# Delta net of a decoder layer: sample tile as first chunk, gates and stores inside the token projection, output norms per pair

## The chip, the cores and the metric

One core of a Trainium2 chip runs the whole program. The metric is device time in microseconds for one execution. The kernel before takes 1897.65 us (median of three runs, 1895.38 to 1902.17).

## The reference, cut to what matters

The program computes one layer of a hybrid decoder for a prompt of 1024 tokens and a sample group of 8 sequences with 8 tokens each: RMS norm, one input projection, three mixers (sparse attention, a gated delta net, a state space mixer), the output projection and an MLP. The change touches the delta net and the projection ahead of it:

```python
def deltanet_mix(qkv, a, b, z, conv_buf, s0, conv_w, a_log, dt_bias, norm_w):
    ...
    beta = jax.nn.sigmoid(b.astype(f32))
    g = -jnp.exp(a_log.astype(f32)) * jax.nn.softplus(a.astype(f32) + dt_bias.astype(f32))
    o, s_new = gated_delta_chunked(q, k, v, g, beta, s0.astype(f32))
    o = rmsnorm(o, norm_w) * jax.nn.silu(z.astype(f32).reshape(B, L, DN_HEADS, DN_DV))
...
def gated_delta_chunked(q, k, v, g, beta, s0):
    ...
    gc = jnp.cumsum(g...)                       # per chunk
    decay = jnp.where(tri, jnp.exp(gc_i - gc_j), 0.0)
    a_mat = jnp.where(strict, (beta k) @ k^T * decay, 0.0)
    sol = lax.linalg.triangular_solve(a_mat + eye, rhs, left_side=True, lower=True)
    u, w = sol[..., :dv], sol[..., dv:]
    def step(S, xs):
        v_new = u_i - w_i @ S
        o_i = (q_i * exp(g_i)) @ S + a_qk @ v_new
        S = S * exp(g_last) + (k_i * exp(g_last - g_i))^T @ v_new
        return S, o_i
```

(Index bookkeeping is written out as products here.) There are four heads of 64 channels. The prompt starts from a zero state; each sample sequence starts from its own state, which is also returned.

## The kernel before, in words

The rows of all tokens lie in nine tiles: tiles 0 to 7 are the prompt, 128 rows each, and tile TS = 8 holds the 64 rows of the sample group. The program is a row of blocks; within a block every engine runs its own list of instructions, ordered by hand, with semaphores between them, and a block ends on all engines together. The blocks that matter here:

- `project` called by `token_projection` (name `kvp`, lines 394 to 396 for the matmuls, 522 for the copies): a product of the normalised input with four chunks of 264 weight columns; the 36 units (chunk, tile) take 24 matmuls of three kinds each. Columns 0 to 767 are keys and values of the attention (`m.kv`), the other 288 are `m.small`: attention gates (24), the delta net's a and b (4 each) and z (256). ScalarE copies the even units, VectorE the odd ones. Behind its last copy ScalarE's queue issues the stores of the keys and values (lines 529 to 536, function `stores`), and the block ends when they are issued.
- `delta_net` (from line 1140). SyncE loads parameters and constant tables (1250 to 1255), then the page table and the 16 pages of the attention's cache (1262), and once all tiles' rows are read the sample states (1265). Gates (1337 to 1348, 1444 to 1462) take z through SiLU, softplus and exponentials for all tiles at once, with cumulative sums on TensorE (1649 to 1653). Then tile by tile: decay rows (1687), rows turned out of the convolution's result (1664), normalised and scaled (`normalise` 1471 to 1478 on VectorE, `scale` 1297 to 1303 on GpSimd), turned (1675), products of keys and queries (1703), decayed (1507).
- The triangular solve is done in levels, for pairs of tiles, `PAIRS = [(0, 1), (2, 3), (4, 5), (6, 7), (TS,)]`: seven levels for a full pair, three (`SLEVELS`) for the sample tile, whose blocks are 8 x 8. A level is `lower` on TensorE, a copy on ScalarE, `joined` on TensorE, an update on VectorE (1541 for level 0, 1561 for level 6, 1553 for the sample tile). Between these steps of pair p, the next pair is prepared, and the chained part of pair p - 1 runs, tile by tile: `w_products` (1766), `v_products` (1776 to 1785), `s_products` (1791, 1796), `next_state` (1521), `take_o` (1528).
- Behind the last pair: `finish` squares, sums, takes the root by a power on GpSimd (1333), multiplies with the norm's weight, the root and SiLU(z), for tiles 0 to 5, 6 and 7, and TS; the sample tile's masked products with its eight states (1836 to 1860); `turn_rows` (1823) and `keep_rows` (1430) put the result into `m.mixT`.

In the trace the names `dn_...` are tiles of the delta net, `tokens` holds `m.kv` and `m.small`, and `ps` are the banks of the matmul memory.

## Time and profile before

| | us |
|---|---|
| median of three runs | 1897.65 |
| profiled execution, its own time | 1897.29 |
| its span in the trace | 1895.4 |
| PE busy in the span | 1690.9 (89%) |
| DVE, ACT, POOL busy | 876.1, 517.3, 322.0 |
| mean granted clock of TensorE | 0.906 |

The engines are PE (TensorE, matmuls), PEld (its weight loads), DVE (VectorE), ACT (ScalarE), POOL (GpSimd) and SP (SyncE, which only issues transfers here); a q behind the name is the queue, where transfers are issued. Granted clock 1.0 is 2.4 GHz and 0.5 is 1.2 GHz. Times inside the trace count from the start of the span. A row of a timeline gives start, duration, engine, line, operation, what it writes and reads with shapes, how often; brackets give the idle time before it and what ended it, where "issue" means that the engine waited for nothing the profile shows. Busy times are sums over a stage; an engine can be idle without cost when another one sets the pace.

### The profile page before, as it was taken

How to read it: one execution, taken by the hardware profiler on the slowest of the kernel's cores; microseconds unless marked ns; L12 is line 12 of the kernel's file. 1: busy time of each engine (PE TensorE's matmuls, PEld its weight loads, DVE VectorE, ACT ScalarE, POOL GpSimd, SP SyncE). 2: the span in 40 equal slices, each digit the busy share in tenths (PEclk: the TensorE clock that was granted, in tenths of full speed). 3: DMA queues.
4: the chain of work that ended last, by engine and by line, in shares of the span. 5: the costliest groups of instructions: out<-in, count | busy, mean ns of one | idle time of the engine just before them, and what ended most of it. 6: DMA issues, size and time to landing. Idle time of an engine off the chain costs nothing. (4 is left out here: it accounts for less than half of the span.)

```text
span 1895.4 us, 34835 instructions
## 1 busy us (share of the span) xinstructions
PE 1690.9 (89%) x15219; PEld 1521.4 (80%) x15219; DVE 876.1 (46%) x1742; ACT 517.3 (27%) x1043; POOL 322.0 (17%) x291
## 2 busy tenths in 40 slices
PE   6999889648886676689998999999999999999998
PEld 5999889647775565467778999999999999999996
DVE  5950631033534321667754264444444444444447
ACT  6212421022211221566653042111111111111112
POOL 2010020022211000567760001111111111111110
PEclk8999999857865655799999999999999999999999
DMA  4010110240000202000003101111111111111102
GB/s 149 24 37 12 59 46 24 71 131 3 4 31 2 76 1 88 1 1 2 1 2 117 45 23 56 45 45 45 45 45 45 45 45 45 45 45 45 45 23 95
DMA packets 28498, 81.14 MB, mean 43 GB/s; under 512 B 6922, under 2 KB 15226, under 8 KB 23066
## 3 DMA queue, kind: packets, MB, share of 16 engines
q1 hardware_dynamic: 25810, 73.03, 11.5%
q10 hardware_dynamic: 1976, 4.92, 0.7%
q8 instruction: 119, 1.95, 0.4%
q0 software_dynamic: 560, 0.97, 0.2%
q14 instruction: 33, 0.27, 0.0%
HBM read 70.89 MB, written 10.12 MB: 43 GB/s over the span
## 5 line engine op out<-in xcount | busy, mean ns | idle before, releaser
L394 PE MATMUL ps<-mlp_mix_hi,mlp_w_hi 128*128 128x360 f32 (+1 forms) x768 | 252.5, 329 | 0.0
L396 PE MATMUL ps<-mlp_mix_hi,w_lo 128*128 128x360 f32 (+1 forms) x768 | 252.3, 329 | 0.0
L395 PE MATMUL ps<-mixT_lo,mlp_w_hi 128*128 128x360 f32 (+1 forms) x768 | 251.5, 328 | 0.0
L2650 DVE TENSOR_TENSOR x<-x,ps 128x512 f32<-128x512 f32 (+1 forms) x288 | 180.6, 655 | 137.7 <-PE ps L396 137.0
L2630 POOL TENSOR_TENSOR mlp_rect<-mlp_rect 128x360 f32<-128x360 f32 (+1 forms) x96 | 77.5, 807 | 775.4 <-ACT mlp_rect L2572 775.4
L394 PE MATMUL ps<-mlp_w_hi,mlp_hid_hi_lo 128*128 128x512 f32 x512 | 202.1, 395 | 0.0
L396 PE MATMUL ps<-mlp_w_hi,mlp_hid_lo 128*128 128x512 f32 x512 | 202.1, 395 | 0.0
L395 PE MATMUL ps<-w_lo,mlp_hid_hi_lo 128*128 128x512 f32 x512 | 202.1, 395 | 0.0
L2572 ACT ACTIVATE mlp_rect<-ps 128x360 f32<-128x360 f32 (+1 forms) x96 | 45.5, 474 | 554.2 <-PE ps L396 551.3
L2212 POOL TENSOR_SCALAR pa_probs<-pa_probs,pa_fac 128x640 f32<-128x640 f32 (+7 forms) x96 | 158.7, 1666 | 187.9 <-DVE pa_fac L2139 187.9
L2690 DVE TENSOR_TENSOR mlp_hid_lo<-mlp_rect,mlp_hid_hi_lo 128x368 fp32r<-128x368 f32 (+1 forms) x64 | 53.1, 830 | 234.8 <-ACT mlp_hid_hi_lo L2578 234.8
L394 PEld LDWEIGHTS ps<-mlp_mix_hi,mlp_w_hi 128*128 128x128 f32 x768 | 144.5, 188 | 0.8
L395 PEld LDWEIGHTS ps<-mixT_lo,mlp_w_hi 128*128 128x128 f32 x768 | 144.4, 188 | 0.7
L396 PEld LDWEIGHTS ps<-mlp_mix_hi,w_lo 128*128 128x128 f32 x768 | 144.1, 188 | 0.0
L396 PEld LDWEIGHTS ps<-mlp_w_hi,mlp_hid_lo 128*128 128x128 f32 x512 | 96.5, 188 | 22.5
L395 PEld LDWEIGHTS ps<-w_lo,mlp_hid_hi_lo 128*128 128x128 f32 x512 | 96.5, 188 | 22.5
L394 PEld LDWEIGHTS ps<-mlp_w_hi,mlp_hid_hi_lo 128*128 128x128 f32 x512 | 96.4, 188 | 22.4
L2224 ACT ACTIVATE pa_probs<-pa_probs,pa_nm 128x640 f32<-128x640 f32 (+7 forms) x128 | 92.5, 728 | 9.9 <-DVE pa_nm L2128 9.8
L2640 DVE TENSOR_TENSOR w_lo<-w_raw,mlp_w_hi 128x2048 fp32r<-128x2048 f32 x36 | 82.4, 2288 | 25.0 <-ACT mlp_w_hi L2547 25.0
L394 PE MATMUL ps<-kvp_whi,h_hi 128*128 128x264 f32 x288 | 82.8, 287 | 6.3 <-DVE kvp_wlo L476 6.3
L2071 PEld LDWEIGHTS ps<-ident,pa_probs 128*128 128x128 f32 x528 | 57.4, 142 | 37.5 <-issue 33.1
L2071 PE MATMUL ps<-ident,pa_probs 128*128 128x128 f32 x528 | 70.4, 280 | 18.7 <-issue 15.7
(491 smaller groups left out, 3411.5 us busy)
## 6 DMA issues: line engine op xcount, KB each, us to landing
w_raw<-in_w_up SPq DMA_DIRECT2D x16, 1024.0 KB, 4.9
w_raw<-in_w_down SPq DMA_DIRECT2D x16, 1024.0 KB, 4.9
feat_raw<-in_w_feat SPq DMA_DIRECT2D x12, 512.0 KB, 3.6
uT<-in_w_token SPq DMA_DIRECT2D x4, 1056.0 KB, 5.0
ck<-in_cache_nsa SPq DMA_DIRECT2D x16, 256.0 KB, 2.9
w_raw<-in_w_out SPq DMA_DIRECT2D x4, 1024.0 KB, 7.2
x<-in_x_prompt SPq DMA_DIRECT2D x4, 1024.0 KB, 8.5
out_y_p<-x SPq DMA_DIRECT2D x8, 512.0 KB, 2.6
```

The source lines that it names most:

```text
L394: pe.matmul(out, lhs[0], rhs[0], start=first, stop=False)
L395: pe.matmul(out, lhs[0], rhs[1], start=False, stop=False)
L396: return pe.matmul(out, lhs[1], rhs[0], start=False, stop=last)
L2071: last = pe.transpose(m.ps[:, 4 + st % TURNS, (2 * s + g) * P:(2 * s + g + 1) * P], probs[:, slot(e, g), col:col + P], m.ident[:])
L2212: last = pool.tensor_scalar(probs[:, x, o:o + w], probs[:, x, o:o + w], fac[:, x, b:b + 1], None, ALU.mult)
L2224: act.activation(probs[:, x, o:o + w], probs[:, x, o:o + w], ACT.Exp, bias=nm[:, x, b, pieces(i)[j][1]:pieces(i)[j][1] + 1], scale=-1.0, a ...
L2572: act.activation(rect[:, (rank[u] - 1) % 2, :w], m.ps[:, bank_of(u), :w], ACT.Relu).then_inc(rectified, 1)
L2630: pool.tensor_tensor(part, part, part, ALU.mult).then_inc(rect_squared, 1)
L2640: dve.tensor_tensor(w_lo[:, s, :], w_raw[:, s, :], w_hi[:, s, :], ALU.subtract).then_inc(w_lo_made, 1)
L2650: dve.tensor_tensor(part, part, bank, ALU.add).then_inc(done, 1)
L2690: dve.tensor_tensor(hid_lo[:, g % 2, f, o:o + w], part, hi, ALU.subtract).then_inc(hidden_lo, 1)
```

## The change

`TOKEN_ORDER = (3, 0, 1, 2)`: the token projection takes its last chunk of columns first, so that a, b and most of z are there after nine units. A new class `DeltaGates` does all gate work between the projection's units: loads by GpSimd, `scalar` at units 10, 12 and 18, `vector` at 9, 10, 12, 14 and 17, the five sums on TensorE behind unit 16, in bank 7, which the projection gives up. GpSimd multiplies SiLU(z) with the norm's weight there. The stores move to SyncE's list and follow the copies they need; the twelve large ones of the prompt become three. In the delta net, chunk j = 0 is the sample tile and j = 1 to 8 are tiles 0 to 7, `PAIRS = [(0,), (1, 2), (3, 4), (5, 6), (7, 8)]`. The sample tile's masks, products and state update stand in the steps of pair 1; its states and masks lie in the memory of the attention's cache, whose loads wait until the states are stored. `finish` becomes `finish_sums`, `roots` and `finish_rows`, once per pair.

```diff
+TOKEN_ORDER = (3, 0, 1, 2)
...
     def stores(sp, evac):
-        sp.wait_ge(evac[0], (len(units) + 1) // 2)
-        sp.wait_ge(evac[1], len(units) // 2)
-        for t in range(TS):
-            sp.dma_start(m.kv_prompt[t * P:(t + 1) * P, :], m.kv[:, t, 0:512]).then_inc(stored, 16)
-            if t >= TS // 2:
-                sp.dma_start(m.win_prompt[(t - 4) * P:(t - 3) * P, :], m.kv[:, t, 512:768]).then_inc(stored, 16)
...
+        sp.dma_start(m.win_sample[:, 0:PAST, :], m.cache_win).then_inc(stored, 16)
+        for t0 in (0, 4):
+            units_done(2 * TILES + t0 + 3)
+            sp.dma_start(m.kv_prompt[t0 * P:(t0 + 4) * P, :].rearrange("(t p) n -> p t n", p=P), m.kv[:, t0:t0 + 4, 0:512]).then_inc(stored, 16)
+        units_done(3 * TILES - 1)
+        sp.dma_start(m.kv_sample, m.kv[:NB * NQ, TS, 0:512]).then_inc(stored, 16)
+        units_done(3 * TILES + TS - 1)
+        sp.dma_start(m.win_prompt.rearrange("(t p) n -> p t n", p=P), m.kv[:, TS // 2:TS, 512:768]).then_inc(stored, 16)
+        units_done(len(units) - 1)
         for b in range(NB):
+            sp.dma_start(m.win_sample[b, PAST:PAST + NQ, :], m.kv[b * NQ:(b + 1) * NQ, TS, 512:768]).then_inc(stored, 16)
...
+class DeltaGates:
...
+    def tensor(self, pe, u):
+        if u != 16:
+            return
+        pe.wait_ge(self.loaded, 16 * self.LOADS)
+        pe.wait_ge(self.g_ready, 1)
+        pe.matmul(bank[:, 0:32], C["upto"][:], g, start=True, stop=True)
...
-        names = ["ones", "ones_s", "upto", "upto_s", "level32", "eye32", "seq_row"]
+        names = ["level32", "eye32"]
...
-        Ss = flat_hT[:, :NB * 2 * P].rearrange("p (b c n) -> p b c n", b=NB, c=2)
+        Ss = flat_ck[:, 0:2048].rearrange("p (b c n) -> p b c n", b=NB, c=2)
...
-        PAIRS = [(0, 1), (2, 3), (4, 5), (6, 7), (TS,)]
-        STEPS = [7, 7, 7, 7, SLEVELS]
+        PAIRS = [(0,), (1, 2), (3, 4), (5, 6), (7, 8)]
+        STEPS = [SLEVELS, 7, 7, 7, 7]
...
             @block.sync
+                sp.dma_start(Ss, m.state_dn).then_inc(s_in, 16)
...
+                sp.wait_ge(ss_ready, H * SP_CHUNKS)
                 for h in range(2):
                     half = slice(64 * h, 64 * h + 64)
+                    for c in range(2):
+                        sp.dma_start(m.dn_sample[half, :, c], Ss[half, :, c, half]).then_inc(stored, 16)
+                sp.wait_ge(stored, 16 * 4)
                 sp.wait_ge(pages_loaded, 16)
                 for j in range(NB * PAGES):
...
             @block.gpsimd
+                def roots(p):
+                    pool.wait_ge(osq, p + 1)
+                    pool.tensor_tensor(part(T1), part(T0), m.minus_half[:, :H * (t1 - t0)], ALU.pow).then_inc(orn, 1)
...
             @block.vector
                     at_step(p, 2, level, [(next_state, c), (take_o, c), (normalise, b)])
+                    if p >= 2:
+                        finish_sums(p - 2)
+                    at_step(p, 3, level, [(take_o, 0 if p == 1 else None), (decayed, a)])
+                    if p == 1:
+                        decay_sample()
                     at_step(p, 4, level, [])
+                    spread_blocks(p)
+                    if p == 1:
+                        next_sample(0)
+                        next_sample(1)
                     at_step(p, 5, level, [(decayed, b), (next_state, d), (take_o, d)])
+                    if p == 1:
+                        next_sample(2)
                     at_step(p, 6, level, [])
+                    if p == 1:
+                        next_sample(3)
+                    if p >= 2:
+                        finish_rows(p - 2)
...
             @block.tensor
+                def sample_s(i):
+                    if i:
+                        pe.wait_ge(ss_ready, H * i)
...
+                for s, piece in enumerate(((w_products, 0), (sample_v,), (sample_o,), (), (sample_s, 0), (sample_s, 1), (sample_s, 2))):
+                    lower(1, s)
+                    if piece:
+                        piece[0](*piece[1:])
+                    at_step(1, s, joined, then)
```

How the instructions move, at three places. First, the border between the token projection and the delta net. Before, on ScalarE, the last stores, the end of the block, and the first gate step:

```order
L532 DMA out_kv_s<-tokens 64x512
L534 DMA out_win_s<-tokens 8x256 x8
L536 DMA out_win_s<-in_cache_win 8x4x16384
L438 UNCONDITIONAL_BRANCH
L1335 UNCONDITIONAL_BRANCH
L1337 ACTIVATE tokens<-tokens 128x9x256
L1339 ACT_TABLE_LOAD
L1339 ACTIVATE dn_gate<-dn_gate 128x36
```

Now, on SyncE, from the projection's weight loads to the delta net's first loads:

```order
L445 DMA uT<-in_w_token 128x2112 x3
L534 DMA out_win_s<-in_cache_win 8x4x16384
L537 DMA out_kv_p<-tokens 128x4x512 x2
L539 DMA out_kv_s<-tokens 64x512
L541 DMA out_win_p<-tokens 128x4x256
L544 DMA out_win_s<-tokens 8x256 x8
L438 UNCONDITIONAL_BRANCH
L1388 UNCONDITIONAL_BRANCH
L1392 DMA dn_level<-in_const 128x160
L1392 DMA dn_eye<-in_const 128x32
L1393 DMA ck<-in_state_dn 128x2048
L1395 DMA ck<-in_const 128x512
```

The stores are off ScalarE; on SyncE all but the last two groups stand ahead of the last units' copies, and only two tables are loaded before the sample states (`ck<-in_state_dn`).

Second, TensorE's products for the sample tile. Before, they stand at the end of the delta net, between two groups of turned output rows (`ident,dn_o`):

```order
L1766 MATMUL ps<-dn_TT,dn_kbg 64x64 x4
L1823 MATMUL ps<-ident,dn_o 128x128 x12
L1836 MATMUL ps<-dn_vb,dn_TT 64x64 x4
L1840 MATMUL ps<-mixT_raw,dn_B 64x128 x16
L1846 MATMUL ps<-mixT_raw,dn_TT 64x128 x16
L1854 MATMUL ps<-dn_vnew,dn_AT 128x128 x16
L1860 MATMUL ps<-dn_vnew,dn_aqkT 64x64 x4
L1823 MATMUL ps<-ident,dn_o 128x128 x4
L1823 MATMUL ps<-ident,dn_o 128x64 x2
```

Now they stand in the first levels of pair 1 (`dn_T,dn_B` are the levels, `ident,mixT_raw` and `ident,dg_gate` rows and decay rows of the next pair):

```order
L1860 MATMUL ps<-dn_featT 128x128 x8
L1878 MATMUL ps<-ident,dn_B 32x32 x32
L1928 MATMUL ps<-dn_TT,dn_kbg 64x64 x4
L1822 MATMUL ps<-ident,mixT_raw 128x128 x6
L1844 MATMUL ps<-ident,dg_gate 128x128 x8
L1878 MATMUL ps<-dn_T,dn_B 32x32 x32
L1967 MATMUL ps<-dn_vb,dn_TT 64x64 x4
L1972 MATMUL ps<-ck 64x128 x16
```

The sample tile's first products follow level 0, and the sixteen with the states follow level 1 of pair 1. The rest follows in the same way, one group for each level.

Third, GpSimd in pair 2, with the semaphores that each instruction waits for. Before, in the pair (4, 5), the next two tiles are scaled one right after the other:

```order
L1297 TENSOR_TENSOR dn_qg<-dn_qk,dn_gate 128x256 [waits dn_turned,dn_gexp,dn_normed]
L1301 TENSOR_TENSOR dn_kdec<-dn_qk,dn_gate 128x256 [waits dn_sprod,dn_wprod]
L1303 TENSOR_TENSOR dn_kbg<-dn_kb,dn_gate 128x256 [waits dn_kb_made]
L1297 TENSOR_TENSOR dn_qg<-dn_qk,dn_gate 128x256 [waits dn_turned,dn_gexp,dn_normed]
L1301 TENSOR_TENSOR dn_kdec<-dn_qk,dn_gate 128x256 [waits dn_sprod,dn_wprod]
L1303 TENSOR_TENSOR dn_kbg<-dn_kb,dn_gate 128x256 [waits dn_kb_made]
L1320 TENSOR_TENSOR dn_B<-dn_ATc,dn_level 128x5x128 [waits dn_bt,dn_packed_a]
```

Now, in pair (3, 4):

```order
L1430 TENSOR_TENSOR dn_qg<-dn_qk,dg_gate 128x256 [waits dn_turned,dn_normed]
L1434 TENSOR_TENSOR dn_kdec<-dn_qk,dg_gate 128x256 [waits dn_sprod,dn_wprod]
L1436 TENSOR_TENSOR dn_kbg<-dn_kb,dg_gate 128x256 [waits dn_kb_made]
L1461 TENSOR_TENSOR dg_gate<-dg_gate,minus_half 128x4 [waits dn_osq]
L1430 TENSOR_TENSOR dn_qg<-dn_qk,dg_gate 128x256 [waits dn_turned,dn_normed]
L1434 TENSOR_TENSOR dn_kdec<-dn_qk,dg_gate 128x256 [waits dn_sprod,dn_wprod]
L1436 TENSOR_TENSOR dn_kbg<-dn_kb,dg_gate 128x256 [waits dn_kb_made]
```

The power for the output norm of pair 0 (`dg_gate,minus_half`, which waits for VectorE's sums) stands between the scaling of the two tiles. In pair 3 the same instruction stands there with eight columns.

## Rows read from the trace of the kernel before

**Rows 1.** Table by stage: us; busy PE, PEld, DVE, ACT, POOL; PE clock, DMA share, GB/s.

```profile
364.00:377.00 13.00, 0.43 (x4) 0.21 (x2) 0.42 (x1) 0.16 (x1) 0.00 (x0) 0.65 0.73 257
377.00:397.00 20.00, 2.68 (x10) 2.43 (x10) 2.85 (x14) 6.99 (x12) 2.87 (x5) 0.50 0.48 155
397.00:422.00 25.00, 15.07 (x142) 13.11 (x143) 9.66 (x22) 4.81 (x15) 9.44 (x10) 0.57 0.41 125
...
459.00:499.00 40.00, 33.69 (x1112) 30.44 (x1106) 18.29 (x46) 9.54 (x27) 9.51 (x10) 0.84 0.02 4
...
537.00:580.00 43.00, 35.09 (x1009) 31.58 (x1006) 11.90 (x32) 6.92 (x20) 3.66 (x5) 0.58 0.10 34
...
602.00:645.00 43.00, 18.98 (x131) 16.69 (x132) 24.13 (x39) 3.74 (x11) 8.73 (x3) 0.68 0.07 14
```

**Rows 2.** Timeline of ScalarE: start, us, what; in brackets the idle time before.

```profile
372.11 3.12 ACTq L534 DMA_DIRECT2D out_win_s<-tokens  x8
...
376.84 2.12 ACT L1337 ACTIVATE tokens<-tokens 128x2304 f32<-128x2304 f32 x1 [14.89 <-PEq L438]
...
644.88 1.28 ACT L1909 ACT_TABLE_LOAD   x1 [1.70 <-PEq L2851]
```

**Rows 3.** Timeline of SyncE's queue.

```profile
380.60 4.60 SPq L1255 DMA_DIRECT2D dn_eye<-in_const  x1
...
387.70 0.34 SPq L1258 DMA_DIRECT2D pages<-in_page_table  x1
390.58 17.24 SPq L1262 DMA_DIRECT2D ck<-in_cache_nsa  x16
...
539.15 0.34 SPq L1265 DMA_DIRECT2D mixT_raw<-in_state_dn  x1
```

**Rows 4.** Timeline of VectorE, end of the token projection and first gate step.

```profile
364.46 0.42 DVE L522 COPY tokens<-ps 64x264 f32<-64x264 f32 x1 [5.37 <-PE ps L396]
388.95 0.20 DVE L1444 TENSOR_TENSOR dn_gate<-tokens,dn_dtb 128x36 f32<-128x36 f32 x1 [24.07 <-DMA dn_normw<-in_norm_w]
```

**Rows 5.** Timeline of TensorE, a gate sum and the decay rows.

```profile
394.95 0.61 PE L1653 MATMUL ps<-dn_gm,dn_ones 64*128 64x32 f32 x2
...
397.12 3.78 PE L1687 MATMUL ps<-ident,dn_gate 128*128 128x128 f32 x16 [1.56 <-ACT dn_egl_s L1348]
```

**Rows 6.** Timeline of VectorE: first levels, last levels, last state step.

```profile
422.00 0.41 DVE L1541 TENSOR_TENSOR dn_T<-dn_eye,ps 128x256 f32<-128x256 f32 x1
...
459.30 0.41 DVE L1541 TENSOR_TENSOR dn_T<-dn_eye,ps 128x256 f32<-128x256 f32 x1
...
537.11 0.41 DVE L1541 TENSOR_TENSOR dn_T<-dn_eye,ps 128x256 f32<-128x256 f32 x1
...
579.52 0.68 DVE L1561 TENSOR_SCALAR dn_TT<-ps 64x512 f32<-64x512 f32 x1 [3.06 <-PE ps L1753]
...
591.75 0.35 DVE L1553 TENSOR_TENSOR dn_T<-dn_T,ps 64x256 f32<-64x256 f32 x1
...
599.59 1.16 DVE L1521 SCALAR_TENSOR_TENSOR dn_S<-dn_S,dn_gate,ps 64x64 f32<-64x64 f32 x4 [5.96 <-PE ps L1791]
```

**Rows 7.** Timeline of TensorE: a turn, a stop, a chained tile, sample products.

```profile
518.56 0.63 PE L1675 MATMUL ps<-ident,dn_qk 128*128 128x128 f32 x4
...
546.62 0.33 PE L1746 MATMUL ps<-dn_T,dn_U 32*32 32x32 f32 x8 [3.08 <-issue]
...
593.32 1.12 PE L1766 MATMUL ps<-dn_TT,dn_kbg 128*64 128x128 f32 x8 [1.76 <-DVE dn_S L1521]
...
619.94 5.65 PE L1840 MATMUL ps<-mixT_raw,dn_B 128*64 128x128 f32 x32
```

**Rows 8.** Page of the profile, DMA queues: packets, MB, share of 16 engines.

```profile
q8 instruction: 119, 1.95, 0.4%
```

**Rows 9.** Timeline of GpSimd: the scaling of a tile, the power over eight columns.

```profile
516.67 0.85 POOL L1297 TENSOR_TENSOR dn_qg<-dn_qk,dn_gate 128x256 f32<-128x256 f32 x1 [12.69 <-DVE dn_qk L1471]
...
620.45 2.01 POOL L1333 TENSOR_TENSOR dn_gate<-dn_gate,minus_half 128x8 f32<-128x8 f32 x1 [9.76 <-DVE dn_gate L1611]
```

More of the change, by code:

```diff
@@ new lines, in next_sample @@
+                def next_sample(i):
+                    dve.wait_ge(ss_prod, i + 1)
+                    upd = m.ps[:, W0, :].rearrange("p (b c n) -> p b c n", b=2, c=2)
+                    for h in range(H):
+                        half = slice(64 * (h % 2), 64 * (h % 2) + 64)
+                        blk = Ss[half, 2 * i:2 * i + 2, h // 2, half]
+                        dve.tensor_tensor(blk, blk, upd[half, :, h // 2, half], ALU.add).then_inc(ss_ready, 1)
+                dve.wait_ge(tables, 16 * len(names))
@@ L1653, in _, with rows_of @@
-                pe.matmul(bank[:, 128:160], C["ones"][:64, :], gm[:].rearrange("p b h -> p (b h)"),
-                          start=True, stop=True).then_inc(sums, 1)
-                pe.wait_ge(gexp, 4)
-                def rows_of(k):
-                    n = ROWS[k]
-                    if k:
-                        pe.wait_ge(feat_out, 3 * k)
+                def rows_of(j):
+                    n, t = rows_in(j), tile(j)
+                    low, high = row_banks(j)
+                    if j >= 2:
+                        pe.wait_ge(feat_out, 3 * j)
@@ L1709, in lower @@
                     if s == 0:
-                        pe.wait_ge(b_ready, sum(len(x) for x in PAIRS[:p + 1]))
+                        pe.wait_ge(b_ready, PAIRS[p][-1] + 1)
                     else:
@@ L1806, in _ @@
+                sample_s(3)
+                for p in range(2, len(PAIRS)):
                     (a, b), (c, d) = following(p), chained(p)
```

910 lines of the change are left out of this document (511 added, 399 removed).

## The prediction

> **What bounds the kernel now.** I read the table by stage first, then each engine's timeline at the stage borders, then the waits and the DMA queue. TensorE is the engine of the whole program, but the change touches only the stretch from the end of the token projection to the end of the delta net, 364 to 645 us, and there it is not saturated: in the table by stage [rows 1] PE is busy 0.43 us of the 13 between 364 and 377, 2.68 of the next 20, 15 of the next 25, then 34 and 35 of the 40 and 43 us of two of the pairs of tiles, and 19 in the last 43. So five pieces follow one another, each with its own limit, and I cost each by itself.
>
> First, 364 to 397. ScalarE's queue still has to issue the projection's stores; eight small ones of them alone take 3.12 us, and its first delta net instruction stands at 376.84 [rows 2]. Only then does SyncE begin the small loads; one of them holds its queue for 4.60 us [rows 3], and VectorE waits for the last of the gate parameters until 388.95 [rows 4]. Then come the gates, and TensorE's first real step, the decay rows, starts at 397.12 [rows 5]. Second, 397.12 to 422.00: the first two tiles are prepared with nothing beside them. Third, the pairs: the marks "first level of a pair" stand at 422.00, 459.30 and 537.11, and the last level of the last full pair at 579.52 [rows 6]. Each pair is a loop of hand-offs (TensorE, ScalarE, TensorE, VectorE), and TensorE is busy some 34 us of it. Fourth, 579.52 to 645: the sample tile's levels, its masks and products and the output norms, one behind the other; VectorE is the busier engine there, 24 of the 43 us after 602 [rows 1].
>
> **The start, -23.6 us.** The stores leave ScalarE. SyncE now issues all but the window rows of the last chunk before the last unit; what remains behind it are the eight small stores, 3.1 us [rows 2]. The gate sums on TensorE move into the projection, where it never idles: five groups like the row of 0.61 us at the half clock [rows 5], at full clock about 1.5 us in all, so the last unit ends at 366.0 instead of 364.5, its copy at 366.4. Then 3.1 us of stores, 0.8 to leave the block (ScalarE's eight stores end at 375.23, one more follows, and its next instruction starts at 376.84 [rows 2]), 0.8 for two table loads like the 0.34 us one, and 2.5 until they land; a small load lands in under 2.9 us when nothing is queued before it (387.70 to 390.58) [rows 3]. TensorE starts at 373.5 instead of 397.12. The gates' vector and scalar steps, the seven loads that GpSimd issues and its product with the norm's weight cost nothing: VectorE is idle 5.37 us between two copies of the projection [rows 4], ScalarE as long, and TensorE has seven banks ahead. If that cover failed, the price would be the 8.2 us from 388.95 to 397.12 again [rows 4, 5].
>
> **The first tiles, +18.3 us.** Before, two tiles take 24.9 us (397.12 to 422.00). Now the sample tile comes first and tiles 0 and 1 are prepared around its three levels. The engines' busy times of this stretch add to 39 us over four engines [rows 1], so it is a chain of hand-offs, little overlapped. I add two thirds of one tile's 12.4 us for the half-height sample tile, 8.3, and 10 for its three levels, which before ran from just after 579.52 to 591.75 beside chained products [rows 6]. That gives 43.2, so the first full pair starts at 416.7, 5.3 us earlier than before. Lower bound: the two fully overlap, 33; upper: nothing overlaps, 48.
>
> **The four full pairs, +8.3 us.** Before, they take 157.5 us: 37.3 (nothing chained behind it), 77.8 for the middle two, 42.4 for the last [rows 6].
> - The pair that carries the sample tile. It replaces a middle pair's two chained tiles. The sample's products are longer: 5.65 us for one of three groups [rows 7], and about 15 for all (the 19 us of TensorE in the last stage [rows 1] less the turning of finished rows); two chained tiles take about 10 at that clock. VectorE gets masks, a decay and 16 additions instead of two state updates, some 5 us more of work in a pair where it is busy 18 of 40 us; but the four state chunks pass through one bank, so each waits for the one before. 38.9 + 5.6 = 44.5. It could be 41 (all in idle time) or 50 (the chunks in full on the path).
> - The next pair carries the cache loads. Before, SyncE issued them from 390.58 over 17.24 us [rows 3], when TensorE had few instructions to fetch. Now they wait for the sample states, whose place they take, and start as this pair does. The nearest row is the one large load before inside the pairs, at 539.15: TensorE then stands still for 3.08 us before 546.62, ended by "issue", that is, with no semaphore missing [rows 7]. Bounds: nothing, or one such stop for each instruction packet; the page of the profile counts 119 instruction packets [rows 8] for TensorE's 30,438 weight loads and matmuls, so one each 256; 17.24 us of a pair hold some 480 matmuls [rows 1], four packets, 12.3 us. Each piece is a quarter of that load in bytes, so I take 4. **A rule against this:** the Trainium skill (Runtime: NRT & Kernel Launch, Instruction fetch mechanics) says that fetching is hidden by the rate at which instructions are issued. By that rule the term is nothing and the sum 4 us lower; the 3.08 us row speaks against it.
> - Output norms. GpSimd now raises the sums of squares to a power between the scaling of a pair's two next tiles, and VectorE makes the sums just before. For eight columns the power takes 2.01 us [rows 9]. In the third pair VectorE's step before the sums ends at 517.4 (0.7 after the scaling starts at 516.67); with 1.6 of sums (two passes over 512 columns of some 0.7 us each) and the power, the scaling (0.85 us) [rows 9] would end at 522, and TensorE's turn of that tile stands at 518.56 [rows 7]: 3.4 us late. In a pair that runs slower there it is less, down to nothing. I take 1 us for the pair with the sample's four columns and 2 for the next. The second half of each norm falls behind the last level, where VectorE waits for TensorE anyway.
> - The last pair has nothing to prepare: 42.4 less the 3.08 us stop and 2.8 for the sample tile's own preparation, 36.5.
> The sum is 44.5 + (38.9 + 0.5 + 4 + 1) + (38.9 - 0.5 + 2) + 36.5 = 165.8; the 0.5 is the first middle pair's excess over the mean. So the last level starts at 582.5.
>
> **The tail, -40.6 us.** Before, 65.4 us from 579.52 to 644.88 [rows 2, 6]. Now, after the last level (0.7): two chained tiles of 7.4 each (593.32 to 600.75, the end of the state step) [rows 6, 7]; the last output's copy, sums, power and products, 0.4 + 1.6 + 2.0 + 1.4 with gaps, 5.6; turning and copying two tiles 2.0; leaving the block 1.7 [rows 2]. That is 24.8, and the earlier tiles turn beside it. The sample tile's levels, its products, two of three norms and the wait for its state are gone from here.
>
> **Sum.** -23.6 + 18.3 + 8.3 - 40.6 = -37.6 us. The profiled execution took 1897.29 us, 0.4 below the median, which gives 1859.7, so I predict 1860. Nothing after the block changes; the cache pages land long before their first use.
>
> **Rivals.**
> 1. Better than that, 1850: the three sample levels hide in the preparation (-5), and the loads and the power stop nothing (-5). For it: PE idles 10 of 25 us while the first tiles are prepared. Against: the 3.08 us row. Chance 0.20.
> 2. The small stores and the window store still stand before the tables: SyncE's queue stalls as it did for 4.60 us [rows 3], and the tables land behind half a megabyte of window rows, 2 us at the 257 GB/s of the stores before [rows 1]. The start gains 17 and the time is 1866. This is the case in which the change doesn't take the stores off the path. Chance 0.07.
> 3. The clock stays low. In the last pair before, the mean granted clock is 0.58 (between its levels of 1.2 and 2.4 GHz) and the pair takes 42.4 us although half of its preparation is missing; at 0.84 the first of the full ones takes 39 to 40 [rows 1]. With the clock low, a full pair costs 42.4 less the stop of 3.1, plus about 8 for the preparation that is missing there: 47. Three of them in place of 44.5, 44.4 and 40.4 add 11.7, which gives 1871. Chance 0.10.
> 4. **Slower:** every one of the 16 cache loads stops TensorE for 3.08 us, as the one load did. 16 x 3.08 = 49.3 in place of 4 gives 1905. At 14 stops the gain is used up (37.6 + 4 = 41.6 us), and only the full 16 leave the band of no change. Against: 17 us hold only four instruction packets. Chance 0.03.
> The forecast itself, within 7 us of 1860, has 0.60.
>
> **Numbers.** The range, 1846 to 1876, holds the forecast, rival 1 with 4 us below it, rivals 2 and 3 with 5 us above the latter, and leaves rival 4 out, and of rivals 1 and 3 what goes further, together less than 0.2. A measurement of this kernel tells 0.3%, 5.7 us, from no change. Faster 0.96; same 0.02 and slower 0.02, from rival 4 and from rivals 3 and 4 together.
>
> **What would show it.** Right: no delta net load before 369 but TensorE's decay rows near 373.5; the first full pair at 417, the last level near 582, the block's end near 607; TensorE's projection longer by 1 to 2 us. Step by step wrong: decay rows after 378 (rival 2); sample pair over 50 us; stops by "issue" of 3 us in the pair after it and a clock of 0.5 from there (rivals 3, 4); TensorE's turn of the second tile waiting for GpSimd by under 0.5 us (then the norms were free). The forecast is wrong as a whole if the time lies above 1880 or if the tail after the last level is over 35 us.

## The result, and the profile after

The changed kernel takes 1864.45 us (median of four runs, 1864.05 to 1867.81) against 1896.62 for the one before; the ratio is 0.9829, 95% interval 0.9806 to 0.9852. The forecast was 1860. The profiled execution took 1864.05 us, its span is 1862.2.

The table by stage of the kernel after, cut at the marks of the forecast (columns as in [rows 1]): the end of the projection to the decay rows, the first tiles, the pair with the sample tile, the three pairs behind it, the tail.

```profile
364.00:377.94 13.94, 6.34 (x53) 6.13 (x52) 0.86 (x2) 0.39 (x1) 2.81 (x5) 0.81 0.29 92
377.94:419.93 41.99, 24.44 (x296) 20.98 (x298) 19.16 (x43) 7.55 (x25) 13.46 (x15) 0.54 0.05 18
419.93:467.43 47.50, 41.14 (x1143) 37.35 (x1142) 26.36 (x59) 8.75 (x25) 11.35 (x10) 0.79 0.01 3
467.43:510.98 43.55, 36.31 (x1100) 32.61 (x1096) 19.50 (x50) 9.54 (x27) 10.27 (x11) 0.77 0.41 112
510.98:552.18 41.20, 32.66 (x1094) 29.10 (x1092) 20.80 (x51) 10.04 (x28) 10.89 (x11) 0.87 0.02 4
552.18:591.17 38.99, 32.15 (x944) 29.56 (x944) 10.09 (x26) 4.87 (x12) 1.64 (x1) 0.50 0.01 3
591.17:613.86 22.69, 15.54 (x90) 13.12 (x90) 11.02 (x23) 4.79 (x13) 3.27 (x2) 0.73 0.02 4
```

Set against the marks before [rows 2, 5, 6]:

| piece | before | after | difference | forecast |
|---|---|---|---|---|
| decay rows start at | 397.12 | 377.94 | -19.2 | -23.6 |
| first tiles | 24.88 | 41.99 | +17.1 | +18.3 |
| four full pairs | 157.52 | 171.24 | +13.7 | +8.3 |
| tail | 65.36 | 22.69 | -42.7 | -40.6 |
| end of the block | 644.88 | 613.86 | -31.0 | -37.6 |

The spans differ by 33.2 us, so 2.2 more were won behind the block, where nothing is changed. Something is off ahead of it as well. VectorE's first step of the token projection, in its timeline before:

```profile
255.38 2.36 DVE L476 TENSOR_TENSOR kvp_wlo<-uT,kvp_whi 128x2112 fp32r<-128x2112 f32 x1 [2.29 <-ACT kvp_whi L459]
```

and after, with the projection's last copy:

```profile
259.63 2.36 DVE L476 TENSOR_TENSOR kvp_wlo<-uT,kvp_whi 128x2112 fp32r<-128x2112 f32 x1 [2.29 <-ACT kvp_whi L459]
...
370.38 0.43 DVE L526 COPY tokens<-ps 64x264 f32<-64x264 f32 x1 [5.37 <-PE ps L396]
```

The same work came 4.25 us later, and from there to the last copy it is 110.75 us instead of 109.08 [rows 4]: 1.7 us for the gate sums, forecast 1.5. The 4.25 us arose far ahead, where the clock fell for longer (TensorE's table by stage, in rows of 6 us). Before:

```profile
108.00:114.00 6.00, 6.00 (x101) 0.54 0.01 3
114.00:120.00 6.00, 6.00 (x34) 0.89 0.00 0
```

After:

```profile
108.00:114.00 6.00, 6.00 (x120) 0.50 0.01 3
114.00:120.00 6.00, 6.00 (x47) 0.50 0.31 87
```

In the twelve experiments below, which all leave that part alone, the same VectorE step stands between 255.39 and 259.62, and what follows the block takes 1245 to 1253 us. The time of one execution therefore moves by several us with no cause in the change, and I compare stages, and the **stretch** from the projection's last copy to the block's end: 280.42 us before, 243.48 after, -36.9; with the 1.7 of the sums -35.3, where the forecast was -37.6.

SyncE's queue after, to be read against [rows 3]:

```profile
370.88 2.68 SPq L544 DMA_DIRECT2D out_win_s<-tokens  x8
374.06 0.37 SPq L1392 DMA_DIRECT2D dn_level<-in_const  x1
374.48 0.43 SPq L1392 DMA_DIRECT2D dn_eye<-in_const  x1
...
473.21 16.87 SPq L1406 DMA_DIRECT2D ck<-in_cache_nsa  x16
```

The eight small stores take 2.68 us behind the last copy, two table loads follow, and the cache loads run in the second full pair. TensorE's timeline shows what the decay rows waited for, the landing of the second table:

```profile
377.94 1.11 PE L1844 MATMUL ps<-ident,dg_gate 64*64 64x64 f32 x8 [7.60 <-DMA dn_eye<-in_const]
```

TensorE's waits in the delta net, 377 to 614 us (in total, times, longest; all the rows with "issue", and the one for the scaled rows):

```profile
PE ps L1878 <- issue: 4.4, 5, 1.4
PE ps L1903 <- issue: 4.3, 3, 2.2
PE ps L1834 <- POOL dn_qg L1430: 3.7, 4, 1.9
PE ps L1900 <- issue: 3.5, 3, 1.9
...
PE ps L1883 <- issue: 0.9, 1, 0.9
```

The stops by "issue" add to 13.1 us; before, they add to 14.4. Where they lie can be counted. The page of the profile has 119 instruction packets of 16 KB for TensorE's 30,649 records (weight loads, products, semaphore waits and the like), one for some 256 of them. Between 400 and 612 us the fourteen traces of this case have 130 places where TensorE stands still for over 0.6 us with no semaphore missing, and at every one of them the count of records up to the stop is 194 more than a multiple of 256. Two of them, one multiple apart, in TensorE's timeline before:

```profile
431.01 0.57 PE L1721 MATMUL ps<-dn_T,dn_B 32*32 32x32 f32 x43 [0.86 <-issue]
...
434.46 0.26 PE L1743 MATMUL ps<-dn_U,dn_T 32*32 32x32 f32 x2 [1.44 <-issue]
```

So the stops lie a whole number of packets apart; not every packet has one. That TensorE waits there for the next packet to arrive is the plain reading; no run tested it.

In the pair of the sample tile VectorE looks late (its timeline):

```profile
445.55 5.00 DVE L1750 TENSOR_TENSOR ck<-ck,mixT_raw 64x512 f32<-64x512 f32 x4
450.59 0.69 DVE L1676 TENSOR_TENSOR dn_T<-dn_T,ps 128x512 f32<-128x512 f32 x1
```

Four operations that decay the sample states take 5.00 us, beside GpSimd's work, and level 4 follows at 450.59 with no idle time. In the tail the last state step ends at 605.76, the second chained tile takes 6.3 us, and the next block begins at 613.86 (before, [rows 2, 6]).

### The profile page after: what moved, and what is told of

Same layout as the page of the kernel before. It is cut to its first block and busy times, and to the rows that moved or that the text cites. A ratio compares the mean times of both kernels' runs of the same rounds, so it can differ in the third digit from the quotient of the medians.

```text
span 1862.2 us, 34853 instructions
## 1 busy us (share of the span) xinstructions
PE 1692.9 (91%) x15219; PEld 1523.6 (82%) x15219; DVE 882.3 (47%) x1761; ACT 516.9 (28%) x1043; POOL 331.1 (18%) x303
## 5 line engine op out<-in xcount | busy, mean ns | idle before, releaser
L2263 PEld LDWEIGHTS ps<-ident,pa_probs 128*128 128x128 f32 x528 | 58.1, 143 | 37.6 <-issue 33.3
```

Source lines behind the costliest of these rows:

```text
L2263: last = pe.transpose(m.ps[:, 4 + st % TURNS, (2 * s + g) * P:(2 * s + g + 1) * P], probs[:, slot(e, g), col:col + P], m.ident[:])
```

## The experiments

In brackets stand the ratio to the kernel before, timed alongside, and its 95% interval. "Stretch" is as above, from the one profiled execution of each kernel; the changed kernel has 243.48. Differences of a few us in the medians were read with the stretch beside them, for the reason given.

**1. Stores back on ScalarE.**

```diff
-        sp.dma_start(m.win_sample[:, 0:PAST, :], m.cache_win).then_inc(stored, 16)
-        for t0 in (0, 4):
-            units_done(2 * TILES + t0 + 3)
...
+        sp.wait_ge(evac[0], (len(units) + 1) // 2)
+        sp.wait_ge(evac[1], len(units) // 2)
+        for t0 in (0, 4):
...
-            {"sync": stores, "gpsimd": ...
+            {"stores": stores, "gpsimd": ...
```

> The changed kernel (1864.45 us) with all stores of keys and values back on ScalarE's queue behind its last copy. Theory of the prediction (the stores gate the start twice: by the time of their issue and by their bytes in front of the delta net's first tables): issue ends 2.5 us later than SyncE's last store does now, and the tables land behind 2.6 MB of stores, some 6 us later, so TensorE's decay rows move from 377.9 to 386 and the time is 1872. Rival (only the issue counts, small loads pass the large stores): decay rows near 380.5, time 1867.

The edit also moves the copy of the window's old rows (`cache_win`, 2.1 MB) from the first place among the stores to the last.

1878.99 us (0.9903, 0.9875 to 0.9930), stretch 259.81. ScalarE's queue, SyncE's queue and TensorE in three timelines:

```profile
370.06 6.27 ACTq L537 DMA_DIRECT2D out_win_s<-tokens  x8
```

```profile
378.29 0.49 SPq L1386 DMA_DIRECT2D dn_eye<-in_const  x1
```

```profile
390.77 1.11 PE L1838 MATMUL ps<-ident,dg_gate 64*64 64x64 f32 x8 [24.88 <-DMA dn_eye<-in_const]
```

The stores matter more than either theory said: from the last copy (365.92) to the decay rows it is 24.9 us instead of 7.6, +17.3. The issue takes 10.7 us on ScalarE (the eight small ones 6.27, on SyncE 2.68), and the second table, issued at 378.29, lands 12.5 us later instead of 3.5 (374.48 to 377.94). It is not the keys and values that it lands behind: between 366 and 377 their queue moved 2.82 MB, which is all of them. What moves beside the tables is the copy of the window's old rows, issued at 376.36. The DMA view from 377 to 390 (packets, MB, share of 16 engines; then KB and us to landing):

```profile
q10 hardware_dynamic: 40, 2.10, 41.7%
...
dn_level<-in_const SPq DMA_DIRECT2D x1, 80.0 KB, 3.5
```

The changed kernel issues this copy at 295.68, long before. No run moves the copy alone, and the first table landed in 3.5 us beside it, so how much of the 12.5 us is the copy's stays open. The way from the last copy to the decay rows is 25.1 us shorter in the changed kernel than before (32.66 to 7.56); 17.3 of these are the stores, the old rows' copy among them.

**2. Gate chain behind the projection.** SiLU and its product with the norm's weight stay in the projection.

```diff
-            {"sync": stores, "gpsimd": lambda pool, _: dg.gpsimd(pool), "scalar": dg.scalar, "vector": dg.vector, "tensor": dg.tensor},
+            {"sync": stores, "gpsimd": lambda pool, _: dg.gpsimd(pool), "scalar": dg.silu},
...
+                DG.tensor(pe, 16)
+                pe.wait_ge(DG.gexp, 4)
                 pe.wait_ge(tables, 16 * len(names))
```

> The changed kernel with the gate chain (all but SiLU) run at the head of the delta net instead of between the projection's units. Theory of the prediction (cover gone costs the 8.2 us of the chain in full): decay rows 8.2 us later less the 1.7 us that the gate sums add to the projection, +6.5, time 1871. Rival (TensorE waits at this place for the tables anyway, from 374.1 to 377.9, so the chain is hidden behind them for 3.8 us): decay rows near 380.6, +2.7, time 1867.

1867.26 us (0.9836, 0.9809 to 0.9863), stretch 248.00; the projection is 1.5 us shorter. TensorE's timeline:

```profile
382.58 1.11 PE L1856 MATMUL ps<-ident,dg_gate 64*64 64x64 f32 x8 [1.55 <-ACT mixT_raw L1224]
```

The decay rows start 13.7 us behind the last copy (368.90) instead of 7.6: +6.1, less 1.5. So the rival's mechanism holds, with +4.6 in place of its +2.7: the chain is 9.9 us long (372.68 to 382.58), and the tables' landing hides the first 3.8 of it. The 8.2 us of the prediction were the price with nothing beside it. The first tiles take 1.8 us of this back (40.17 us instead of 41.99, at a clock of 0.63 instead of 0.54), so that the stretch is longer by 4.5 only and the net loss is 3.0, near the rival's 2.7 and the median's 2.8.

**3. A shorter start.**

```diff
                 sp.dma_start(pages[:], m.a["page_table"]).then_inc(pages_loaded, 16)
+                for b in range(NB):
+                    sp.dma_start(m.win_sample[b, PAST:PAST + NQ, :], m.kv[b * NQ:(b + 1) * NQ, TS, 512:768]).then_inc(m.sem("proj_stored"), 16)
...
-                pool.wait_ge(tables, 16 * len(names))
                 scale(0)
                 scale(1)
+                pool.wait_ge(tables, 16 * len(names))
                 pack(0)
...
-                dve.wait_ge(tables, 16 * len(names))
                 bound(PAIRS[0])
...
+                dve.wait_ge(tables, 16 * len(names))
                 at_step(0, 0, level, [(normalise, 2)])
...
-                pe.wait_ge(tables, 16 * len(names))
```

> The changed kernel with the eight small window stores behind the delta net's own first loads, and with the wait for the two tables put where they are first used, instead of ahead of everything. Theory (what stands between the last copy and the decay rows is the 2.7 us of store issue and the 3.8 us until the tables land): decay rows at 371.5 instead of 377.9, and the first full pair 6.4 us earlier, time 1858. Rival (the first tiles are then held by GpSimd, which fills its zero tiles until 377 before it scales the first tile): the decay rows come early, but the first full pair gains 3 us at most, time 1861.

1853.45 us (0.9764, 0.9736 to 0.9791), stretch 236.09, -7.4. The decay rows start 0.75 us behind the last copy:

```profile
368.05 0.65 PE L1842 MATMUL ps<-ident,dg_gate 64*64 64x64 f32 x8 [0.79 <-PEq L438]
```

and the first tiles take 41.09 us, 0.9 less than in the changed kernel, so the tiles are not held back by GpSimd (its zero tiles now start at 368.01 too). The 6.8 us of the start are won in full; the median fell by more, 11 us, and the stretch says that 7.4 of them are this edit's.

**4. Cache loads at the end.**

```diff
+                sp.wait_ge(s_ready, TS - 1)
                 sp.wait_ge(pages_loaded, 16)
                 for j in range(NB * PAGES):
```

> The changed kernel with the sixteen cache loads issued behind the last but one state step (near 598) instead of in pair 2. Theory of the prediction (loads slow TensorE's instruction fetch by 4 us in that pair): pair 2 takes 39.6 instead of 43.6 us, time 1860.5. Rival (the stops by issue are there in pair 3 too, 5.7 us with no load running, so the loads have no part in them; this is also what the Trainium skill's Runtime: NRT & Kernel Launch, Instruction fetch mechanics, would make of the term, namely nothing): pair 2 stays at 43.6 within 1 us, the sum of the stops stays near 13 us, time 1864 or more if the loads are late for their first use at 631.

1866.19 us (0.9840, 0.9811 to 0.9869), stretch 247.29. The table by stage (TensorE only: busy, clock, DMA share, GB/s), the pair that had the loads, the next, the last:

```profile
465.09:507.67 42.58, 36.78 (x1101) 0.78 0.09 16
507.67:549.23 41.56, 34.33 (x1092) 0.83 0.01 3
549.23:584.05 34.82, 25.45 (x944) 0.75 0.02 4
```

The pair shrinks by 1.0, not by 4, and with 42.58 us it lies inside the 41.7 to 45.9 of the nine other runs that leave the loads and this pair's work alone. The stops by "issue" in the delta net still add to 12.6 us (13.1), and all that are over 0.6 us fit the same count as above: the loads have no part in them. Two surprises came with it. The last pair took 34.8 instead of 39.0, at a clock of 0.75 instead of 0.50, of which more below. And the tail grew from 22.7 to 31.5, as ScalarE's timeline shows, because SyncE needs until 610.5 to issue the loads, and the state's store behind them, and the block ends on all engines:

```profile
615.54 1.28 ACT L2102 ACT_TABLE_LOAD   x1 [10.55 <-PEq L3044]
```

**5. The norm's power behind both scalings.**

```diff
-                        if p >= 2:
-                            roots(p - 2)
                         scale(b)
+                        if p >= 2:
+                            roots(p - 2)
```

> The changed kernel with the power of each output norm behind the scaling of both next tiles, not between them. Theory of the prediction (1 us in pair 2, 2 us in pair 3): those pairs take 42.6 and 39.2 us, time 1861.4. Rival (the turned tile is not what the level waits for; TensorE has other work there): TensorE waits less for the scaled rows (3.7 us in all now) but the pairs shrink by under 0.5 us each, time 1864.

The two pairs:

```profile
467.75:510.62 42.87, 36.01 (x1100) 0.78 0.42 114
510.62:551.65 41.03, 33.98 (x1094) 0.83 0.02 4
```

43.55 became 42.87 and 41.20 became 41.03; TensorE's waits for the scaled rows went from 3.7 to 3.5 us, and in these two pairs they had been 0.2. The rival is right in the profiled execution: 0.7 and 0.2 us are less than the same pairs vary by in other runs, and no wait accounts for them. The stretch is 243.48 to the hundredth. Yet the median is 1856.85 us (0.9778, 0.9761 to 0.9796), 7.6 under the changed kernel, with an interval that doesn't touch the changed kernel's (0.9806 to 0.9852), and the profiled run is the slowest of its four. What the other three did I can't see. Whether the edit gains something that this one execution doesn't show stays open.

**6. Without the sample states' update.**

```diff
-                for s, piece in enumerate(((w_products, 0), (sample_v,), (sample_o,), (), (sample_s, 0), (sample_s, 1), (sample_s, 2))):
+                for s, piece in enumerate(((w_products, 0), (sample_v,), (sample_o,), (), (), (), ())):
...
-                    if p == 1:
-                        decay_sample()
```

The calls of `next_sample` and `sample_s(3)` are gone too, and the waits for the states' update now wait for earlier steps. So the cache loads start inside this pair.

> The changed kernel without the decay of the sample states, without the sixteen products of their update and without the sixteen additions: this part of the computation is left out. It measures what the state's update costs in the pair that carries the sample tile. Theory (VectorE is late: level 4 starts without idle time behind the decay of 5.0 us, and the four chunks wait for one another): the pair shrinks from 47.5 to 41, time 1858. Rival (the update lies in idle time and the pair is long by the sample tile's 32 longer products): 46 or more, time 1863.

1847.91 us (0.9745, 0.9721 to 0.9769), stretch 232.72. The pair:

```profile
416.49:459.61 43.12, 35.34 (x1108) 0.78 0.28 71
```

It took 43.12, between the two: the update costs 4.4 us there. TensorE's busy time fell by 5.8 and VectorE lost some 10 us of work, so this run alone doesn't say which of them it was. Most of the other 6.4 us by which the stretch is shorter lie in the next pair (40.74 instead of 43.55, clock 0.84 instead of 0.77) and in the last (35.52 instead of 38.99, clock 0.60 instead of 0.50), whose work is the same.

**7. The decay ahead of the next tile's masks.**

```diff
-                    at_step(p, 3, level, [(take_o, 0 if p == 1 else None), (decayed, a)])
+                    at_step(p, 3, level, [(take_o, 0 if p == 1 else None)])
                     if p == 1:
                         decay_sample()
+                    if a is not None:
+                        decayed(a)
```

> The changed kernel with the decay of the sample states ahead of the masks of the next tile's products, so that it no longer runs beside GpSimd's packing. Theory (the four operations take 5.0 us because both engines work on the same memory at once; alone they take 0.68 each, and level 4 waits for VectorE): they take 2.8 us in all, level 4 comes 2.2 us earlier and the pair takes 45.3, time 1862.3. Rival (they take as long as they do for another reason, as two operands that are read along the states): 5 us again, and no change, 1864.5, or up to 2 more since the masks come later.

1863.92 us (0.9822, 0.9805 to 0.9840), stretch 243.20. VectorE's timeline:

```profile
441.93 2.77 DVE L1750 TENSOR_TENSOR ck<-ck,mixT_raw 64x512 f32<-64x512 f32 x4
...
448.37 0.69 DVE L1676 TENSOR_TENSOR dn_T<-dn_T,ps 128x512 f32<-128x512 f32 x1 [1.52 <-PE ps L1905]
```

Half of the theory held. Away from GpSimd's packing the decay takes 2.77 us, as said, and the packing takes 1.54 us instead of 2.04. But now VectorE waits 1.52 us for TensorE, and level 4 comes 30.73 us into the pair, where it had been 30.66. A row without idle time had misled me: both engines were ready at about the same moment, and the pair stayed long (48.74).

**8. The sample tile's products with the queries left out.**

```diff
-                    for b in range(NB):
-                        for c in range(2):
-                            pe.matmul(obank[:, c * P:(c + 1) * P], qgm[:, c, b, :], Ss[:, b, c, :],
-                                      start=b + c == 0, stop=False, skip_group_check=True)
```

> The changed kernel without the products of the sample queries with the eight states (3.5 us of TensorE at full clock in the pair with the sample tile): this part of the sample tile's output is left out. Theory, formed after the run with the decay moved (TensorE's own work at a clock of 0.75 to 0.79 sets this pair, VectorE only seemed late): the pair shrinks from 47.5 by the 3.5 us, to 44, time 1861. Rival (the chain of the four state chunks on VectorE sets it): under 1 us, 47.

1862.30 us (0.9813, 0.9790 to 0.9835), stretch 242.90. The pair took 49.75 us, 2.25 more. Neither theory said so. The reason is in two timelines, VectorE's levels 2 and 3 of that pair, 15.19 and 24.10 us into it (18.02 and 22.55 in the changed kernel):

```profile
434.65 0.69 DVE L1676 TENSOR_TENSOR dn_T<-dn_T,ps 128x512 f32<-128x512 f32 x1 [2.54 <-PE ps L1903]
443.56 0.69 DVE L1676 TENSOR_TENSOR dn_T<-dn_T,ps 128x512 f32<-128x512 f32 x1 [4.00 <-PE ps L1903]
```

and TensorE's table by stage:

```profile
431.46:435.46 4.00, 2.92 (x192) 1.00 0.02 4
435.46:439.46 4.00, 2.11 (x16) 0.68 0.02 4
439.46:443.46 4.00, 3.50 (x199) 0.50 0.02 4
```

Level 2 came 2.8 us earlier; then TensorE idled, part of it a stop by "issue" of 2.16 us, the clock fell to 0.50, and level 3 took 8.9 us instead of 4.5. In the changed kernel the clock is 1.00 from 423.93 to 443.93. It falls to 0.50 at 27.6 to 28.7 us into this pair in the changed kernel and ten of the other runs, at 21.0 us in run 12, and here at 17.4 us. The stop of 2.16 us lies at an instruction count like that of the others; with the products in place there is none over 0.6 us at that count. So work taken off TensorE was answered by a stop and an earlier fall of the clock. The fall is far from anything else on record; the pair's length is not, as 49.75 us is 0.7 above the longest of the others (49.06).

**9. Extra products in the last pair**, 28 of them.

```diff
+                            pe.matmul(m.ps[:, G0, 0:128], m.ident[:], m.ident[:], start=True, stop=True)
...
                         at_step(p, s, lower, first)
+                        fill(p, 2)
                         at_step(p, s, joined, then)
+                        fill(p, 2)
```

> The changed kernel with four extra products of 128 x 128 with 128 columns in each level of the last pair, into a bank that nobody reads: work is added, nothing taken away. Theory (the last pair takes 39.0 us because its clock is granted at 0.50 all through, after the small products of the levels, and more columns bring it back): the clock rises above 0.8 in the pair, which takes 33 us in spite of the 28 extra products, time 1858. Rival (the clock does not follow this work): clock 0.5, and the extra products add 0.3 us each, 8 us, time 1872.

1859.28 us (0.9791, 0.9770 to 0.9812), stretch 239.48. Last pair and tail:

```profile
550.52:585.10 34.58, 30.25 (x996) 0.88 0.02 4
585.10:605.35 20.25, 13.82 (x94) 0.87 0.02 4
```

39.0 and 22.7 became 34.6 and 20.3, 6.9 us, with 28 products more; the theory held and the rival did not. The net is smaller, as the pairs ahead, unchanged, were slower in this run (45.9 and 42.6). The 6.9 us are counted from an execution with a clock of 0.50 in the last pair; four runs without such products (4, 6, 7, 8) had 0.60 to 0.75 and 34.8 to 36.0 us there.

**10. The same products, small** (against run 9).

```diff
-pe.matmul(m.ps[:, G0, 0:128], m.ident[:], m.ident[:], start=True, stop=True)
+pe.matmul(m.ps[0:32, G0, 0:32], m.ident[0:32, 0:32], m.ident[0:32, 0:32], start=True, stop=True)
```

> The 28 extra products of the last pair made small, 32 x 32 with 32 columns, so that the order of instructions and their number are those of the run with the large ones. Theory (what brings the clock back is the work of the large products): clock 0.50, last pair 39 us, tail 22.7. Rival (the number or the place of the instructions shifted something): clock above 0.8 and 34.6 us as with the large ones.

1862.70 us (0.9831, 0.9800 to 0.9861; the range of the runs is 1860.16 to 1871.10), stretch 242.74.

```profile
547.40:586.61 39.21, 32.49 (x990) 0.54 0.01 4
586.61:609.17 22.56, 15.13 (x94) 0.73 0.02 4
```

As without them. Against the large products' 0.88 the number and the place of the instructions do not lift the clock.

**11. Short start and extra products together** (3 and 9).

> The short start and the extra products of the last pair together. Theory (the extra products keep the clock up there): last pair near 34.6 us at a clock of 0.88 again, tail 20.3, first full pair 7 us early, so the stretch from the projection's last copy to the block's end takes 7.4 + 6.8 = 14 us less than in the changed kernel; time 1849. Rival (the high clock of that run was chance, as three other runs without such products had 0.60 to 0.75 in this pair): last pair 39 at 0.50 or above, time 1853 to 1855.

1846.99 us (0.9747, 0.9720 to 0.9773), stretch 229.33, 14.2 less than the changed kernel's, as the theory said. The last pair and the tail again:

```profile
542.02:576.40 34.38, 30.18 (x996) 0.88 0.02 4
576.40:596.62 20.22, 13.83 (x94) 0.87 0.02 4
```

**12. Extra products among the first tiles too**, 35 of them, into a bank that is idle there.

```diff
                 turn(0)
+                fill_first(4)
                 turn(1)
                 grams(0)
+                fill_first(2)
                 decay_rows(PAIRS[1])
+                fill_first(12)
                 grams(1)
...
                 grams(2)
+                pe.wait_ge(t_ready, step_no(0, 2))
+                fill_first(14)
```

> As the run before, with 35 more extra products while TensorE waits for other engines among the first tiles (42 us, 18 of them idle, at a clock of 0.50 to 0.54). Theory (they bring the clock up, and TensorE's own 24 us of work there take 13): the first tiles take 34 instead of 41.5 us, time 1842. Rival 1 (the clock stays low; the extra products fit in the waits): 41.5, as the run before. Rival 2 (the clock comes up but is given back in the pairs behind): the first tiles gain, and the sample pair and the next lose as much.

1847.41 us (0.9722, 0.9693 to 0.9752), stretch 225.58. The first tiles, then the tail:

```profile
370.67:405.80 35.13, 25.90 (x370) 0.90 0.13 44
...
570.77:595.50 24.73, 19.01 (x94) 0.64 0.01 3
```

The theory holds for the first tiles: they take 35.1 instead of 41.1 us, at a clock of 0.90, and the second pair behind the sample's takes 37.9 instead of 41.2. The last pair and the tail give 6.7 of it back: 2.2 in the pair, whose mean clock is 0.87 as in run 11's 0.88, and 4.5 in the tail, at 0.64 instead of 0.87. Neither rival named this place. The medians of runs 11 and 12 are the same, 50 us under the kernel before and 17 under the changed one.

## Why the prediction was right, and where it was not

The time, 1864.45, lies 4.5 us above the forecast and inside its range. The way was right: the start and the tail are where the time was won. That the sum came so near is in part luck. Ahead of the change 4.25 us were lost and behind it 2.2 won, in stages that it doesn't touch. Between them the four pairs took 5.4 us more than forecast, the first tiles 1.2 and the tail 2.1 less. And inside the pairs 7 us were forecast for the cache loads and the norms, which cost nothing that the runs can show; without them the forecast for the pairs would have been 12.4 us too short. These terms stood in for a clock and for a sample pair that the sum had too good.

- **The start, -23.6.** Decay rows were forecast at 373.5 and came at 377.94. Less the 4.25 us by which everything came late ahead of the change they stand at 373.7. Runs 1 and 2 split the term: the stores are worth 17.3, the gates 6.1 less 1.5. The prediction had the order of things right and priced the issue and a bare landing of 2.5 us (3.5 measured); that a table lands only after 12.5 us when the old rows' copy stands ahead of it, is in none of its terms. That the gates cost nothing but 1.7 us on TensorE held: the copies' idle time is 5.37 us as before [rows 4].
- **The first tiles, +18.3.** Measured +17.1, 42.0 us, and within 0.1 of that in the seven runs that leave the start alone (4 to 10).
- **Sample pair, 44.5.** Measured 47.5, in other runs of the same pair 47.2 to 49.1. The products were sized about right. TensorE's groups by line in that pair, the three large ones of the sample tile (busy, mean ns, idle before):

```profile
L1994 PE MATMUL ps<-dn_vnew,ck 64*128 64x128 f32 x32 | 6.7, 370 | 1.8 <-DVE ck L1761 1.8
...
L1972 PE MATMUL ps<-ck 128*64 128x128 f32 x32 | 3.7, 274 | 0.0
L1980 PE MATMUL ps<-ck 128*64 128x128 f32 x32 | 3.7, 274 | 0.0
```

  These are 14.1 us, and 16.2 with the small ones, where the prediction had about 15; two chained tiles took 10.0 before. What failed is the step from there to the pair's length, 5.6 us for 5: TensorE is busy 41.1 us, 7.4 more than the 33.7 of a middle pair before [rows 1], at a mean clock of 0.79 instead of 0.84, and the others of its products, which are the same, take part of that. Run 6 took 4.4 us off the pair by leaving out work of both engines. The prediction's own reason for an excess, VectorE's work, found no support in run 7, which made VectorE's decay 2.2 us shorter and the pair no shorter. The chunks through one bank made TensorE wait 1.8 us once. The products of the states' update, the longest of this pair, were not taken out alone, so what the rest of the excess is stays open.
- **Cache loads, 4.** Wrong in its cause. Run 4 shows nothing of it beyond what the pair varies by. By the rule of the Trainium skill (Runtime: NRT & Kernel Launch, Instruction fetch mechanics) fetching is hidden and the term is nothing, which is the better price for the loads. The traces don't bear the rule itself out: the stops lie 256 instructions or a multiple of that apart, and add to 13 us with or without loads. The prediction's count of one packet for 256 instructions was right; what failed is that other transfers make the stops. The 3.08 us before 546.62 [rows 7] was one of a dozen, and its instruction count fits theirs; part of it may still be the load's, as it is the longest of all. The pair had 43.55 against 44.4 forecast, for another reason: a clock of 0.77.
- **Norms, 1 and 2.** Nothing in the profile of run 5, whose median is open as said. The power takes 1.01 and 1.64 us, but TensorE has other work at that point.
- **Last pair, 36.5.** Measured 39.0. The estimate took the pair before, at 0.58 [rows 1], and struck off a stop; the clock was 0.50 throughout, which is the step that failed here. Four other runs without extra products had 0.60 to 0.75 here and 34.8 to 36.0 us, the rest 0.50 to 0.54 and 38.7 to 39.5: no single number was to be had.
- **The tail, -40.6.** -42.7, since the second chained tile took 6.3 and the power 1.64 where I had 7.4 and 2.0.
- **Rivals.** The clock (rival 3) was the one that mattered: not as a state that holds for all pairs, but pair by pair, 0.50 in the last and 0.77 in the one behind the sample's. Rival 2 did not occur: SyncE issued the two tables in 0.37 and 0.43 us; late landings like its own are what run 1 shows. Rival 1 was right on the loads and wrong on the three levels, as the first tiles took 42.0 us and not 38; rival 4 rested on the loads alone and fell with run 4.

## What to carry to other kernels

Ask of each wait ahead of a stage what it really waits for and whether the waiting engine needs it: two waits put where their data are used, and eight small stores put behind the block's first five loads, gave 7 us for no work. Where a run of small instructions stops with nothing missing, count the instructions between the stops before a transfer is blamed. Where TensorE is fed by short hand-offs, price a change in it at either clock, not at the mean, and don't take an engine for the bound because its row shows no idle time; move its work and look whether the next step moves. With executions that differ by several us in unchanged parts, compare the stretch between two marks around the change beside the medians.

## What the runs showed of the hardware

- TensorE's stops of 0.6 to 3.1 us with no semaphore missing lie 256 of its instructions apart, or a multiple of that: all 130 of the fourteen traces, 13 to 14 us in the delta net of the two kernels. Run 4, with 4 MB of loads moved away, has them too.
- The same eight stores of 8 rows were issued in 2.68 us by SyncE, 3 us behind the last large store, and in 6.27 us by ScalarE in run 1, where they stood right behind 2.75 MB in four large stores. That the bytes ahead make the difference is not shown: in the kernel before ScalarE issued them in 3.12 us [rows 2] behind the same 2.75 MB in thirteen stores.
- VectorE and GpSimd slow each other down: 64 x 512 operations that take 0.67 to 0.69 us alone (run 7) took up to 1.93 beside GpSimd's packing, and that took 2.04 instead of 1.54.
- The clock fell from 1.00 to 0.50 at 17.4 us into a pair instead of 21.0 to 28.7 (twelve other executions) when 3.5 us of products were taken out of it (one execution, run 8).
- In the last pair the mean clock was 0.87 to 0.88 in all three runs with 28 useless large products, and 0.50 to 0.75 in the ten other executions of the changed kernel and its variants, the one with small products among them. The useless products saved 6.9 us in runs 9 and 11, counted from the slower case without them, and next to nothing in run 12 (61.3 us for pair and tail against 61.7). What follows the block took 1252.3 and 1253.0 us in runs 9 and 12, the two longest of all, and 1245.7 in run 11, so that the price may in part be paid later is not excluded.
